# Where the turned tiles are scaled, and where norm chains stand among weight splits, in a one-core forward pass

## What is computed

```python
h_x = modulate(rms_norm(x, g[0]), mx[0], mx[1])
...
x = x + mx[2] * rms_norm(y_x, g[1])
x = x + mx[5] * rms_norm(sqrelu_mlp(modulate(rms_norm(x, g[2]), mx[3], mx[4]), mlp_w1[i], mlp_w2[i]), g[3])
```

## Time and profile before

| what | us |
|---|---|
| median of 3 runs | 1723.48 |
| lowest and highest run | 1721.24, 1724.27 |
| span of the profiled execution | 1719.7 |
| TensorE matmul busy in it | 1580.2 (92%) |
| TensorE weight load busy | 1299.4 (76%) |
| VectorE busy | 1107.8 (64%) |
| ScalarE busy | 859.1 (50%) |
| GpSimd busy | 13.2 (1%) |

### The profile page before, as it was taken

How to read it: one execution, slowest core, us unless ns; L and a number is a source line. 1 busy time by engine, 2 the same in 40 slices (tenths; PEclk the granted TensorE clock), 3 DMA queues, 4 the chain that set the end, 5 groups by cost and what they waited for, 6 DMA issues and landing times.

```text
span 1719.7 us, 24221 instructions
## 1 busy us (share of the span) xinstructions
PE 1580.2 (92%) x8754; PEld 1299.4 (76%) x8754; DVE 1107.8 (64%) x1811; ACT 859.1 (50%) x1397; POOL 13.2 (1%) x36
## 2 busy tenths in 40 slices
PE   5989989899999999899669999797888799999999
PEld 3855557888888888777559999685666788889788
DVE  3546654654444456679977676686565769687795
ACT  4335554622222227588865554634342558556572
POOL 2000000000000000000000000000000000000000
PEclk9999999899999999999879999899899799999999
DMA  9388731423333322332326666442220479788792
GB/s 337 102 333 311 278 121 51 147 74 97 94 93 96 96 88 72 99 90 82 122 75 196 185 182 194 123 135 86 74 74 25 158 280 332 273 288 317 261 362 104
DMA packets 195802, 279.71 MB, mean 163 GB/s; under 512 B 12435, under 2 KB 111221, under 8 KB 190589
## 3 DMA queue, kind: packets, MB, share of 16 engines
q1 hardware_dynamic: 194308, 274.21, 47.8%
q0 software_dynamic: 1152, 4.19, 0.6%
q10 hardware_dynamic: 248, 0.09, 0.0%
HBM read 277.40 MB, written 1.05 MB: 162 GB/s over the span
## 4 chain that ended last, share of the span: by engine, by line
PE 70%; DVE 15%; ACT 8%; issue 3%; DMA 2%; SPq 0%; POOL 0%; DVEq 0%; ACTq 0%; POOLq 0%
PE bank L433 61%; DVE weights_lo L406 3%; ACT weights_hi L394 2%; DMA ada_rows_in<-in_ada_w_dram 1%; PE bank L707 1%; PE bank L1314 1%; DVE work L2643 1%; ACT act_hi L501 1%; PE bank L1298 1%; PE bank L1282 1%; ACT turn L505 1%; DVE work L2680 1%; DVE work L2690 1%; ACT work L2014 1%; DVE x_and_ctx L2643 1%
## 5 line engine op out<-in xcount | busy, mean ns | idle before, releaser
L406 DVE TENSOR_TENSOR weights_lo<-stage,weights_hi 128x1024 fp32r<-128x1024 f32 x332 | 394.5, 1221 | 78.3 <-ACT weights_hi L394 74.2
L394 ACT ACTIVATE weights_hi<-stage 128x1024 fp32r<-128x1024 f32 x332 | 337.6, 1056 | 149.6 <-PE bank L433 99.1
L433 PE MATMUL bank<-act_hi,weights_hi 128*128 128x256 f32 (+1 forms) x1040 | 330.2, 318 | 17.9 <-DVE weights_lo L406 9.6
L433 PE MATMUL bank<-act_lo,weights_hi 128*128 128x256 f32 (+1 forms) x1040 | 328.1, 316 | 0.0
L433 PE MATMUL bank<-act_hi,weights_lo 128*128 128x256 f32 (+1 forms) x1040 | 328.0, 315 | 0.0
L433 PEld LDWEIGHTS bank<-act_hi,weights_hi 128*128 128x128 f32 x1040 | 203.2, 195 | 32.8 <-DVE weights_lo L406 11.3
L433 PE MATMUL bank<-weights_hi,ff_hi 128*128 128x512 f32 x560 | 219.4, 392 | 1.9 <-DVE ff_lo L2852 1.9
L433 PE MATMUL bank<-weights_hi,act_hi 128*128 128x512 f32 (+1 forms) x488 | 196.9, 403 | 24.6 <-DVE act_lo L2704 16.0
L433 PE MATMUL bank<-weights_hi,ff_lo 128*128 128x512 f32 x560 | 219.0, 391 | 0.0
L433 PE MATMUL bank<-weights_lo,ff_hi 128*128 128x512 f32 x560 | 218.5, 390 | 0.0
L433 PEld LDWEIGHTS bank<-act_lo,weights_hi 128*128 128x128 f32 x1040 | 203.2, 195 | 11.5
(11 more groups left out here) (395 smaller groups left out, 2051.2 us busy)
## 6 DMA issues: line engine op xcount, KB each, us to landing
stage<-in_mlp_w_dram SPq DMA_DIRECT2D x128, 512.0 KB, 4.0
stage<-in_w_dram SPq DMA_DIRECT2D x96, 512.0 KB, 5.8
ada_rows_in<-in_ada_w_dram SPq DMA_DIRECT2D x40, 1024.0 KB, 5.8
x_and_ctx<-in_w_dram SPq DMA_DIRECT2D x48, 512.0 KB, 5.7
work<-in_w_dram SPq DMA_DIRECT2D x48, 512.0 KB, 6.0
stage<-in_w_in_dram SPq DMA_DIRECT2D x32, 512.0 KB, 4.3
stage<-in_lru_w_in_dram SPq DMA_DIRECT2D x20, 512.0 KB, 4.4
stage<-in_attn_w_qkv_dram SPq DMA_DIRECT2D x12, 512.0 KB, 8.1
```

What stands on the lines that cost most here:

```text
L394: act.eng.activation(whi[u % NRING][:], landing(act, u)[:], ACT.Copy).then_inc(sem("hi_ready"), 1)
L406: dve.eng.tensor_tensor(wlo[u % NRING][:], landing(dve, u)[:], whi[u % NRING][:].bitcast(F32), ALU.subtract).then_inc(sem("lo_ready"), 1)
L433: m = pe.eng.matmul(ps, l, r, start=start and j == 0, stop=stop and j == 2, skip_group_check=True)
```

## The change

The turn with `shift` goes bank by bank: in each group of four slices two stay as they were, and for the other two, in the next bank, VectorE makes the exact value out of PSUM (`exact`) and ScalarE only the high part, once VectorE is done with that bank. `n1b` turns both tiles as one pair. In `n0b` and `n1`, TensorE's transposes of the second pair move: in `first_hidden` ahead of the fourth group for x, in `lru_gelu(1)` between its two units. At five places (twice in `n0b`, in `n1`, `n1b`, `n2`) statistics, sums and norms trade places with splits.

```diff
-        PARTS = {"n0b": PAIRS, "n1": PAIRS, "n1b": SINGLES, "n2": SINGLES, "n3": SINGLES}
+        PARTS = {"n0b": PAIRS, "n1": PAIRS, "n1b": [(0, 1)], "n2": SINGLES, "n3": SINGLES}
...
             for d in range(KT):
-                if d % per == 0:
+                by_dve = shift and d // per % 2 == 1
+                if d % per == 0 and by_dve:
+                    act.eng.wait_ge(*exact_at(tag, part, d // per // 2))
+                elif d % per == 0:
                     act.eng.wait_ge(*turned_at(tag, "pe", part, d + per - 1))
...
+                i = act.eng.activation(hhi[:, d, cols], ps, ACT.Identity, scale=colA[:, d, who:who + 1],
+                                       bias=colB[:, d, who:who + 1])
+                if by_dve:
+                    i.then_inc(*act.mark("turned_hi"))
+                    continue
+                i.then_inc(*act.mark())
+                if d >= 2 * per:
+                    act.eng.wait_ge(*turned_at(tag, "lo", part, d - 2 * per))
...
         def turn_dve(dve, tag, part, shift):
...
+                if shift and d % (2 * per) == 0:
+                    dve.eng.wait_ge(*turned_at(tag, "pe", part, d + 2 * per - 1))
+                    for e in range(d + per, d + 2 * per):
+                        i = dve.eng.tensor_scalar(exact(tag, e), part_src(tag, part, e),
+                                                  colA[:, e, who:who + 1], colB[:, e, who:who + 1], ALU.mult, ALU.add)
...
             def first_hidden(tag, turn, cols, between):
                 u0, views = pe.unit, []
                 for part in range(2):
-                    if part:
-                        between()
                     for m in range(4):
                         if part == 0:
+                            if m == 3:
+                                between()
...
             lru_gelu(0)
-            lru_gelu(1)
-            turn_pe(pe, "n1", 1, lambda tt: Y4[:, tt, :])
+            lru_gelu(1, lambda: turn_pe(pe, "n1", 1, lambda tt: Y4[:, tt, :]))
             lru_rec(0)
...
             turn_act(act, "n0b", 0, True)
+            split_hi(act, 2)
             wo_stats(2)
+            split_hi(act, 2)
             x_stats("n0b", 2, xn_a[:, 0, :])
-            split_hi(act, 4)
             wo_stats(3)
...
-            for m in (1, 2, 3):
+            for m in (1, 2):
                 hidden_act(act, "m0_first", m, "m0f", 0, m, slice(0, TX))
-            split_hi(act, 2)
+            split_hi(act, 1)
             turn_act(act, "n0b", 1, True)
+            hidden_act(act, "m0_first", 3, "m0f", 0, 3, slice(0, TX))
+            split_hi(act, 1)
...
             turn_act(act, "n1", 0, True)
+            sum_stats("m0l", 2, Y4)
+            split_hi(act, 1)
+            x_stats("n1", 2, Y4[:, 2, :])
+            split_hi(act, 1)
+            sum_stats("m0l", 3, Y4)
+            x_stats("n1", 3, Y4[:, 3, :])
             split_hi(act, 2)
...
+            for tt in TWO:
                 x_stats("n1b", tt, xn_a[:, tt, :])
...
+            split_hi(act, 1)
             sum_stats("m1l", 0, Y2)
-            split_hi(act, 2)
+            split_hi(act, 1)
             x_stats("n2", 0, Y2[:, 0, :])
-            sum_stats("m1l", 1, Y2)
-            x_stats("n2", 1, Y2[:, 1, :])
             split_hi(act, 1)
             s.wait_ge(*norm_at("n2", "col", 1))
             turn_act(act, "n2", 0, False)
+            sum_stats("m1l", 1, Y2)
+            x_stats("n2", 1, Y2[:, 1, :])
```

More of the change, by code:

```diff
@@ L455, in tile_at, with exact_at, exact @@
             return sem(f"tile_{what}"), ahead + tt + 1
+        def exact_at(tag, part, pair):
+            ahead = sum(len(PARTS[t]) for t in list(PARTS)[:list(PARTS).index(tag)])
+            assert all(len(b) == 4 for b in TURN_BANKS[tag])
+            return sem("turned_exact"), 2 * (ahead + part) + pair + 1
+        def exact(tag, d):
+            at = {"n0b": 5120, "n1": 5120, "n1b": 8192}[tag] + TX * (d % 2 + d // 4 * 2)
+            return WORK[:, at:at + TX]
         def turned_at(tag, what, part, d):
-            return sem(f"turned_{what}"), 16 * list(PARTS).index(tag) + KT * part + d + 1
+            ahead = sum(len(PARTS[t]) for t in list(PARTS)[:list(PARTS).index(tag)])
+            return sem(f"turned_{what}"), KT * (ahead + part) + d + 1
         def part_cols(tag, part):
@@ L933, in mlp_last_y_pe, with y_added_dve @@
                         mm.then_inc(*pe.fill((tag, "yl", n, tt)))
-        def y_added_dve(dve, tag, tt, Y):
+        def y_added_dve(dve, tag, tt, Y, between=None):
             for n in range(2):
+                if n and between:
+                    between()
                 dve.eng.wait_ge(*dve.filled((tag, "yl", n, tt)))
@@ L1400, in lru_gelu @@
                 for m in (0, 1):
+                    if m and between:
+                        between()
                     wh, wl = unit_begin(pe, (KT, P))
@@ L2163, in _ @@
             turn_act(act, "n1b", 0, True)
-            turn_act(act, "n1b", 1, True)
             split_hi(act, 3)
@@ L2567, in _ @@
             split_lo(dve, 2)
-            for m in (1, 2, 3):
+            for m in (1, 2):
                 hidden_dve(dve, "m0_first", m, m, slice(0, TX))
-            split_lo(dve, 2)
+            split_lo(dve, 1)
             turn_dve(dve, "n0b", 1, True)
+            hidden_dve(dve, "m0_first", 3, 3, slice(0, TX))
+            split_lo(dve, 1)
             for m in range(4):
@@ L2623, in _ @@
             turn_dve(dve, "n1", 0, True)
-            split_lo(dve, 2)
-            for tt in (2, 3):
-                last_sum(tt)
-                x_new_dve(dve, "n1", tt, gated_b[:, tt % 2, :])
-                xn_dve(dve, "n1", tt, Y4[:, tt, :])
-                split_lo(dve, 1)
+            last_sum(2)
+            split_lo(dve, 1)
+            x_new_dve(dve, "n1", 2, gated_b[:, 0, :])
+            split_lo(dve, 1)
+            last_sum(3)
+            xn_dve(dve, "n1", 2, Y4[:, 2, :])
+            x_new_dve(dve, "n1", 3, gated_b[:, 1, :])
+            split_lo(dve, 1)
+            xn_dve(dve, "n1", 3, Y4[:, 3, :])
+            split_lo(dve, 1)
             turn_dve(dve, "n1", 1, True)
@@ L2733, in _ @@
                 x_new_dve(dve, "n1b", tt, Y2[:, tt, :])
+            for tt in TWO:
                 xn_dve(dve, "n1b", tt, xn_a[:, tt, :])
             turn_dve(dve, "n1b", 0, True)
-            turn_dve(dve, "n1b", 1, True)
             split_lo(dve, 3)
```

42 lines of the change are left out of this document (19 added, 23 removed).

## The result

The changed kernel takes 1702.35 us (median of 4 runs, 1701.35 to 1705.35); the kernel before 1722.99 us in the runs beside it (1721.24 to 1724.27). The ratio is 0.9874, 95% interval 0.9858 to 0.9891: 20.6 us faster, where 20.7 was forecast, at 1702.8. The profiled execution took 1701.48 us, its span 1699.8.

What follows compares the result with a forecast made beforehand. The prediction took TensorE's stands at the five edited places, 26.6 us together, and clock falls after them as the bound. Terms -9.5 + 3.3 - 6.6 - 7.9 = -20.7 gave span 1699.0, time 1702.8, range 1696.5 to 1710.5.

Steps and rivals of the forecast that it cites:

- The turn: Turning a pair: ScalarE makes 12 instructions instead of 16, last low half 6.0 us after the start, 1.9 us saved per pair.
- The rival that it is dear: In the turns, VectorE's scale-and-shift with two column operands out of PSUM is slow; at 2.1 us each, 1735; chance 0.05.
- this hold, at 1.0 us: Context pair's turn at n0b: VectorE begins at 312.0, which holds ScalarE's third slice 1.0 us.
- n0b, -9.5: Attention output to feed-forward 0: two splits ahead of tile 2's norm chain, no stand or clock fall near 299 us; 9.5 us saved.
- n1, +3.3: First and second pair at n1: tile 3 ready 0.4 us later, half a gelu group behind the transposes; 3.3 us lost.
- The walk through the round trips: Chain at n1: VectorE waits for ScalarE's high half at each moved split; steps sum to 20.1 us, tile 3 ready at 680.8.
- n1b, -6.6: At n1b: both tiles normalised by 887.5, last low half at 894.4, first hidden group ends earlier; 6.6 us saved.
- n2, -7.9: At n2: transposes 4.5 us sooner, tile 1's product earlier, 10.3 us less 2.4 for a fallen clock; 7.9 us saved.
- I take it as falling: At n2: TensorE's clock falls at stands of 1.2 and 1.9 us, costing 2.4 us.
- The rival with the clock up: At n2: the clock stays up, price 2.4 us, giving 1700.4; chance 0.30.
- The 3.8 us carried over from span to median: Whole kernel before: span 1719.7 lies 3.8 us under the median 1723.48; added to span 1699.0 for the forecast time.
- Loads as the wait: Splits moved forward ask for data sooner; n1b and n2 each give half their term back (3.3 + 4.0), 1710.1; chance 0.14.

Runs made afterwards that it cites:

- scalar_turns_all: Changed kernel with VectorE's share of the turn taken back: ScalarE makes all 16 instructions of a pair, VectorE only the subtractions; 1711.4 us.
- n1_splits_behind_order_back: Changed kernel with n1's splits moved out of the steps of the chain and TensorE's order at n1 as before the change; median 1695.7 us.
- n1_turn_order_back: Changed kernel with only TensorE's order at n1 as before: both gelu groups, then the second pair's transposes; median 1701.66 us.

## Why the prediction was right, and where it wasn't

- **The turn.** ScalarE makes 12 instructions with one every 0.45 us, and the first pair's last low half ends 6.0 us after the start (289.19, 295.2), as forecast. The instruction that no row had shown, scale-and-shift out of PSUM with two column operands, takes 539 ns (534 to 545 over its 20), against the 477 of the earlier trace rows and the 480 taken. The rival that it is dear, deciding at 1.5 us, is out. "1.9 us saved per pair" is confirmed in sum but not per pair: at n0b the saving of 2.57 us is 1.8 us of earlier start handed on from the first pair's turn through the chain, and only 0.8 us from the context pair's own turn, because there VectorE came late:

```profile
315.48 1.48 ACT L516 ACTIVATE act_hi<-bank,col_shift,col_scale 128x256 fp32r<-128x256 f32 x3 [0.98 <-DVE work L535]
```

  The prediction had named this hold, at 1.0 us. It isn't of one mind on the saving, which it puts at 1.9 us here and at 1.6 where n1 begins.
- **n0b, -9.5: measured -9.24.** Clock 1.00 in every window from 296 to 325 us, three groups ahead of the transposes and the fourth behind them. The transposes stand at 309.77, which less the late start of 2.45 us is 307.3 (forecast 307.5), and VectorE begins the context turn at 314.45, or 312.0 (312.0).
- **n1, +3.3: measured +1.3, and +2.4 as a mean of five.** The walk through the round trips gave 20.1 us for the chain, and the row says 20.1; the stand was forecast at 6.3 us (the prediction's own terms give 6.2) and is 0.49 + 5.67. Mis-sized is what lies behind it: the second pair's own faster turn was left out of the sum, and scalar_turns_all puts 1.1 us on VectorE's share in this stretch. The prediction also didn't ask what the old order would have done with the new turn: it would have gained 3.7 us (190.52 to 186.78). So the edit at n1 costs 6.2 us, nearly a third of what the whole change brought. As an estimate from the rows, 1.9 of them are the later tile 3 (27.8 against 26.0 us from the first pair's transposes), 2.4 TensorE's order, and the rest, some 2, the fall of clock at the long stand, which the old order no longer has.
- **n1b, -6.6: measured -6.17.** Both tiles normed at 882.1 us (forecast 887.5, less the 5.5 us of shift that n0b and n1 left: 882.0), last low half 889.2 (888.9). The prediction's own ends for the first hidden group (894.9 to 896.1, against 901.7) give 5.6 to 6.8, and it took 6.6. Not all of it is waiting: in the 17 us from just ahead of the first transposes the clock was 0.50 before (884.5 to 901.5 us) and 0.85 now (880 to 897). xn of tile 0 took 0.79 us and of tile 1 0.86 beside GpSimd, 0.75 alone:

```profile
879.75 0.79 DVE L589 TENSOR_SCALAR work<-x_and_ctx,tile_cols 128x1024 f32<-128x1024 f32 x1
```

```profile
879.06 0.93 POOL L3279 TENSOR_SCALAR_AFFINE_SELECT x_and_ctx<-x_and_ctx 128x512 f32<-128x512 f32 x1
```

  By the rule of the Trainium skill (SBUF — State Buffer, Summary: rules for kernel authors) the later of the two is fully blocked, if VectorE runs in its two-port mode; no row names the mode. GpSimd's row starts 0.7 us earlier and lasts 0.25 us into VectorE's, so a full block and then 0.75 us would give 1.0; the row says 0.79. GpSimd's times are rough, so this speaks against the rule without settling it; on the sum it had no effect.
- **n2, -7.9: measured -10.41, and in the second profile of the same code -7.71.** The step that failed is "I take it as falling", not as a size but as a statement with one answer. The fall happened in full in five of eleven profiles, in part in three, and not at all in three, the first profile of the changed kernel among them. Both values the prediction worked out, 10.3 and 7.9, occur: 175.81 less 165.4 and less 168.0. The rival with the clock up, with its 0.30, is the other face of the forecast and not another case. The mean of the eleven, 167.0, gives -8.9.
- **The total.** It came out within 0.5 us for a reason that the prediction doesn't contain: places that gave 3.8 us more, and 4.6 us lost at falls of clock where nothing was edited. The second profile of the changed kernel has +1.20, -9.24, +3.02, -6.01, -7.71 and +1.04 us by stretch, -17.7 in all, and there the four places (-19.9) are 0.8 us short of the forecast. The 3.8 us carried over from span to median hide a second piece of luck: in every run with both figures the time is 1.7 to 1.9 us above the span, so some 2 us of the 3.8 are only how far the one profiled execution before lay under its median. That the size of the sum is right is shown; that it was right to 0.5 us is luck.
- **Loads as the wait.** No stand of TensorE on a load appeared at the five places, and the loops kept their pace: this rival is out. ScalarE's long wait for a load behind n2 isn't new (10.24 us before, 9.96 after).

**What stays open.** The end, from n2's second tile on, took 615.9 to 626.8 us with no edit in it, the largest part of the spread of whole times. Its difference lies in the stage between n2 and the router: up to the router's transposes it took 230.6 to 240.1 us, behind them only 385.1 to 387.1. The granted clock goes with it. These windows are this whole stage, first in n1_splits_behind_order_back (end 615.9), then in n1_turn_order_back (625.8); both have the same 1011 matmuls:

```profile
1071.40:1302.00 230.60, 199.12 (x1011) 157.85 (x1011) 152.94 (x305) 96.22 (x172) 0.00 (x0) 0.94 0.28 89
```

```profile
1078.20:1318.30 240.10, 208.01 (x1011) 164.28 (x1011) 152.92 (x305) 96.16 (x172) 0.00 (x0) 0.91 0.27 84
```

VectorE and ScalarE are busy for the same time in both, and TensorE for 8.9 of the 9.5 us more. So the difference of these two is time at half clock. Whether an earlier arrival at that stage makes its falls likelier isn't told by one profile of each kernel, and no kernel was made to keep TensorE busy there.

## What to carry to other kernels

A piece of filler work that two engines make in turn is no filler inside a dependent chain: if the second engine reaches it before the first has made its half, everything behind waits. Put it where its first half is already done (0.67 us was enough at n1), and count for each moved piece which queue reaches it first. When one part of a change makes a stage faster, price the other parts against that new stage and not against the old one; n1's order looked like +1.3 us and cost 6.2.

Where the clock falls in one execution and not in the next, a term has several values with a share each, not one. Verdicts on parts of 2 to 10 us in a kernel of 1.7 ms were to be had from stretches between rows that both traces have, and hardly from the times.

## What the runs showed of the hardware that was not expected

One and the same stand of 2.73 to 2.75 us, in programs equal up to there, goes with a clock of 1.00, 0.86 or 0.72 in the 12 us around it, and two stands of 1.03 and 1.89 us at n2, 1.1 us of transposes between them, with no fall, part of one or a whole one. The fall needs no long stand: in all five whole falls the clock was at half before the second stand was over. A single stand of 1.72 us at n0b shows none in any of the ten profiles that have it. The Trainium skill (TensorE: Matmul & The Clock Gate, What's actually happening) says of a kernel's first matmuls that the point of change depends on a phase that the kernel's start does not reset, so that it varies from run to run. Equal programs with unequal clocks agree with that; no row here shows the phase itself.
